# A two-layer hybrid trunk on one core: modulation sums in four partition groups, part of layer 0's modulation as steps in the prompt tile's chain, and layer 1's first three tiles in one chain

## The chip, the core and the metric

The kernel runs on one core of a Trainium2 chip. The metric is the device time of one execution in microseconds. TensorE (PE), VectorE (DVE), ScalarE (ACT), GpSimd (POOL) and SyncE (SP) each run their own instruction stream in order, and wait for each other and for DMA transfers by semaphores.

## The reference

128 prompt tokens and 512 latent tokens, 1024 wide, all float32, go through two layers. Each layer is a mixer and a mixture of experts (PEER), and each sub-layer is normed, shifted, scaled and gated by six rows of 1024 that come from a condition vector.

```
def modulation(cond, w_mod, b_mod):
    m = jax.nn.silu(cond) @ w_mod + b_mod
    return jnp.split(m[:, None, :], 6, axis=-1)
...
        sh1, sc1, g1, sh2, sc2, g2 = modulation(cond_ctx, w_mod, b_mod)
        h = modulate(xp, n1, sh1, sc1)
        if li % 2 == 0:
            out, s_f, s_b = mixer_ab(h, *mix_ab, s0, s0)
        else:
            q, k, v = attn_qkv(h, l1_w_in, l1_q_norm, l1_k_norm)
            out = context_attention(q, k, v, l1_sink) @ l1_w_out
        xp = xp + g1 * out
        xp = xp + g2 * peer(modulate(xp, n2, sh2, sc2), wq, pkeys, pu, pv)
```

The latent tokens take the same path with their own condition; in layer 1 they attend within a window of 128 to either side and to 128 cached tokens. `peer` picks 128 of 16384 experts for every token (8 heads, 16 each), takes the dot product of the token with each expert's row of `u`, and adds up the rows of `v` weighted by gate times gelu.

## The kernel before, in words

The tokens are five tiles of 128: tile 0 is the prompt, tiles 1 to 4 the latents. Two things run at once.

**The gathers.** POOL issues 1280 indirect DMAs in one fixed order, 128 "slots" for each of the ten pairs of layer and tile. One slot brings, for each of 128 tokens, one expert's `u` and `v` rows (8 KB a token) into a ring of eight places. VectorE takes the dot product (L1522), ScalarE the gelu and the gate (L1543, L1546), and VectorE (L1531) or TensorE (L1557) adds the `v` row. A ring place is free again after that.

**The stages.** A chain of stages per group of tiles computes norm, projection, mixer or attention, output, query and expert selection. The gathers of a tile can start when its selection is done. `Stage` wraps each: `rate` gives how many slots go by per unit of the stage and `lead` how many before it, and `tick` writes those slots' instructions into the engines' streams at that place. At the end of a stage all engines meet (`core.meet`). Layer 0 and the first stages of layer 1 go: prompt, first latent tile, three other latent tiles, `mod1`, then layer 1's prompt chain (`p1`), the chain of two latent tiles (`s1a`), and more.

Before the first selection there are no slots. There `Early` takes their place: 29 steps, ticked into the prompt tile's layer 0 chain by `EARLY_RATES`, norm the four latent tiles and project them (20 steps of eight matmuls, L1870), in the ring's memory, with POOL loading their weights. POOL starts the gathers after the last of them.

`modulation_stage` streams the 1024 x 6144 matrix in 12 chunks of 512 columns (2 MB each). Its matmuls have the 2 condition vectors as stationary and the chunk as moving operand. These lines of SP's stream set when a chunk is loaded; they are the same before and after:

```
            for n in range(CHUNKS + 2):
                if n >= 2:

                    sp.wait_ge(add_done, n - 1)
...
                if n < CHUNKS:
                    if n >= WSLOTS:
                        sp.wait_ge(mm_done, n - WSLOTS + 1)
                    sp.dma_start(w[:, n % WSLOTS].rearrange("p k n -> p (k n)"), wv[n]).then_inc(w_in[n % WSLOTS], 16)
```

Of the kernel before, what the change touches and what calls it, by code (L numbers as in the profile page):

```python
# [19 lines left out]
ALU = mybir.AluOpType  # L20
# [3 lines left out]
P = 128  # L24
D = 1024
# [215 lines left out]
def modulation_stage(core, layer, tag, rate=None):  # L241

    nc, a = core.nc, core.a
    CH, WSLOTS = 512, 2
    CHUNKS = MODW // CH
    with Stage(core, tag, CHUNKS, rate) as s:
        w = s.sb("w", [P, WSLOTS, DK, CH])
        cond = s.sb("cond", [P, DK, 2])
        gate = s.sb("gate", [P, DK, 2])
        act_c = s.sb("silu", [P, DK, 2])  # L250
        m = s.sb("m", [2, 2, CH])
        ps = s.ps("ps", [P, 2, CH])
# [9 lines left out]
        def _(sp):  # L262
            with nc.allow_non_contiguous_dma(reason="two vectors laid onto partitions"):
                sp.dma_start(cond[:, :, 0], a["c_ctx"].rearrange("(k p) -> p k", p=P)).then_inc(cond_in, 16)
                sp.dma_start(cond[:, :, 1], a["c"].rearrange("o (k p) -> p (o k)", p=P)).then_inc(cond_in, 16)
            wv = a[f"l{layer}_w_mod"]
            bias = a[f"l{layer}_b_mod"]
            for n in range(CHUNKS + 2):
                if n >= 2:

                    sp.wait_ge(add_done, n - 1)
                    sp.dma_start(core.env["mods"][:, layer * MODW + (n - 2) * CH:layer * MODW + (n - 1) * CH],
                                 m[:, n % 2, :]).then_inc(stored[n % 2], 16)
# [7 lines left out]
            for i in range(2):  # L281
                sp.wait_ge(stored[i], CHUNKS // 2 * 16)

        @block.scalar
        def _(act):
            act.wait_ge(cond_in, 32)
            nc.scalar.activation(gate[:], cond[:], ACT.Exp, scale=-1.0).then_inc(exp_done, 1)
            for n in range(CHUNKS):
                s.tick("scalar", act, n + 1)

        @block.vector
        def _(dve):
            order = Order(dve, dve_order)
            dve.wait_ge(exp_done, 1)
            order(nc.vector.tensor_scalar_add(gate[:], gate[:], 1.0))
            order(nc.vector.reciprocal(gate[:], gate[:]))
            nc.vector.tensor_tensor(act_c[:], cond[:], gate[:], ALU.mult).then_inc(silu_done, 1)
            for n in range(CHUNKS):
                dve.wait_ge(mm_done, n + 1)
                dve.wait_ge(b_in[n % 2], n // 2 * 16 + 16)  # L300
                nc.vector.tensor_tensor(m[:, n % 2, :], m[:, n % 2, :], ps[0:2, n % 2, :], ALU.add).then_inc(add_done, 1)  # L301
                s.tick("vector", dve, n + 1)

        @block.tensor
        def _(pe):
            pe.wait_ge(silu_done, 1)
            for n in range(CHUNKS):
# [1835 lines left out]
```

## Time and profile before

| | |
|---|---|
| three runs, median (range) | 4568.01 us (4552.75 to 4571.86) |
| the profiled execution | 4567.51 us, its span 4565.7 us |
| busy: PE, DVE, ACT, POOL | 66%, 69%, 32%, 36% |
| DMA over the span | 1570.41 MB, mean 344 GB/s |
| of it the gathers' queue | 1352.35 MB |

The span is that from the first to the last instruction. Shares of busy time are means over stages with different limits; the windows below are taken at stage boundaries.

### The profile page before, as it was taken

How to read it: one execution, taken by the hardware profiler on the slowest of the kernel's cores; microseconds unless marked ns; L12 is line 12 of the kernel's file. 1: busy time of each engine (PE TensorE's matmuls, PEld its weight loads, DVE VectorE, ACT ScalarE, POOL GpSimd, SP SyncE). 2: the span in 40 equal slices, each digit the busy share in tenths (PEclk: the TensorE clock that was granted, in tenths of full speed). 3: DMA queues.
4: the chain of work that ended last, by engine and by line, in shares of the span. 5: the costliest groups of instructions: out<-in, count | busy, mean ns of one | idle time of the engine just before them, and what ended most of it. 6: DMA issues, size and time to landing. Idle time of an engine off the chain costs nothing.

```text
span 4565.7 us, 34270 instructions
## 1 busy us (share of the span) xinstructions
PE 2993.3 (66%) x9427; PEld 1582.5 (35%) x9427; DVE 3142.8 (69%) x6200; ACT 1458.3 (32%) x4102; POOL 1632.0 (36%) x1292
## 2 busy tenths in 40 slices
PE   7668655786677765556655566575678478766665
PEld 1345334345333311234323342243335353322222
DVE  0224556995799856677777677776869678766666
ACT  0211421451223321352325323262258223332232
POOL 0000222233344435343433334333433334455453
PEclk9789777898889987778877788777887789988887
DMA  6433678788899999899988999979988899999998
GB/s 236 157 108 134 237 312 354 273 319 333 344 406 387 399 386 401 333 374 418 392 350 310 368 370 398 384 278 363 418 329 299 330 417 416 381 421 422 409 422 370
DMA packets 234038, 1570.41 MB, mean 344 GB/s; under 512 B 31717, under 2 KB 36009, under 8 KB 58889
## 3 DMA queue, kind: packets, MB, share of 16 engines
q0 software_dynamic: 185472, 1352.35, 73.6%
q1 hardware_dynamic: 48392, 216.06, 12.2%
q8 instruction: 71, 1.16, 0.1%
q14 instruction: 103, 0.84, 0.0%
HBM read 1565.07 MB, written 3.24 MB: 343 GB/s over the span
## 4 chain that ended last, share of the span: by engine, by line
DMA 37%; PE 22%; DVE 22%; issue 7%; ACT 6%; POOL 2%; DVEq 1%; PEld 1%; SPq 1%; PEldq 1%; ACTq 0%; POOLq 0%
DMA core_ring<-in_l_uv,core_experts 21%; PE sum_rows L1557 6%; DVE core_ring L1522 6%; DVE core_yv L1531 4%; DMA mod_w<-in_l_w_mod 3%; PE mod_ps L312 2%; POOL core_ring L1514 2%; ACT L1543 2%; DVEq L156 1%; PE sum_rows L1870 1%; PE p_in_ps L427 1%; PE p_query_pq L1310 1%; PE s0b_out_po L498 1%; DMA p_in_w<-in_l_w_in 1%; DMA s0a_query_w<-in_l_peer_wq 1%
## 5 line engine op out<-in xcount | busy, mean ns | idle before, releaser
L1514 POOL DMA_INDIRECT core_ring<-in_l_uv,core_experts x1280 | 1627.4, 1271 | 2510.1 <-PE sum_rows L1557 1193.0
L1522 DVE CUSTOM_DVE_ANT_0 core_ring<-core_ring,core_hc 128x1024 f32<-128x1024 f32 x1280 | 1549.0, 1222 | 598.8 <-DMA core_ring<-in_l_uv,core_experts 413.6
L1557 PE MATMUL sum_rows<-core_ring,core_diag 128*128 128x512 f32 x2772 | 1539.3, 700 | 632.3 <-ACT core_diag L1549 536.0
L1557 PEld LDWEIGHTS sum_rows<-core_ring,core_diag 128*128 128x128 f32 x2772 | 571.6, 221 | 1495.5 <-ACT core_diag L1549 860.5
L1543 ACT ACTIVATE core_wt<-core_wt 128x1 f32<-128x1 f32 x1280 | 257.5, 201 | 1888.6 <-DVE core_wt L1522 1768.4
L1531 DVE SCALAR_TENSOR_TENSOR core_yv<-core_ring,core_wt,core_yv 128x1024 f32<-128x1024 f32 x587 | 751.7, 1281 | 37.8 <-ACT core_wt L1546 36.5
L1546 ACT ACTIVATE core_wt<-core_wt,core_gates 128x1 f32<-128x1 f32 x1280 | 376.8, 294 | 64.8
L1549 ACT ACTIVATE core_diag<-core_ident,core_wt 128x128 f32<-128x128 f32 x693 | 278.2, 401 | 22.6
L312 PE MATMUL mod_ps<-mod_w,mod_silu 128*2 128x512 f32 x384 | 180.6, 630 | 67.4 <-DMA mod_w<-in_l_w_mod 67.4
L1543 ACT ACT_TABLE_LOAD x117 | 150.1, 1283 | 12.3 <-SPq L166 6.4
L1870 PE MATMUL sum_rows<-core_ring 128*128 128x416 f32 x320 | 118.4, 529 | 2.5 <-ACTq L151 1.5
L301 DVE TENSOR_TENSOR mod_m<-mod_m,mod_ps 2x512 f32<-2x512 f32 x24 | 16.2, 675 | 144.3 <-PE mod_ps L312 144.3
L312 PEld LDWEIGHTS mod_ps<-mod_w,mod_silu 128*2 128x2 f32 x384 | 32.6, 88 | 214.4 <-issue 160.6
L1522 DVE DVE_READ_ACCUMULATOR2_ANT core_wt<- 128x1 f32 x1280 | 104.0, 81 | 0.0
L1811 POOL DMA_DIRECT2D core_ring<-in_l_w_in x5 | 2.7, 538 | 274.6 <-PE sum_rows L1870 274.6
L1234 ACT ACT_TABLE_LOAD x72 | 92.4, 1283 | 16.2 <-SPq L166 10.6
L1310 PE MATMUL s0b_query_pq<-s0b_h_hT,s0b_query_w 128*128 128x384 f32 x256 | 88.0, 507 | 9.1 <-DMA s0b_query_w<-in_l_peer_wq 6.6
L1310 PE MATMUL p_query_pq<-p_h_hT,p_query_w 128*128 128x128 f32 x512 | 65.3, 290 | 29.3 <-DMA p_query_w<-in_l_peer_wq 29.3
L1870 PEld LDWEIGHTS sum_rows<-core_ring 128*128 128x128 f32 x320 | 61.6, 195 | 54.7 <-issue 54.0
L1310 PEld LDWEIGHTS p_query_pq<-p_h_hT,p_query_w 128*128 128x128 f32 x512 | 62.7, 204 | 33.9 <-DMA p_query_w<-in_l_peer_wq 33.4
L1310 PE MATMUL s1c_query_pq<-s1c_h_hT,s1c_query_w 128*128 128x256 f32 x256 | 61.3, 401 | 12.4 <-DMA s1c_query_w<-in_l_peer_wq 6.8
L1310 PEld LDWEIGHTS s0b_query_pq<-s0b_h_hT,s0b_query_w 128*128 128x128 f32 x256 | 50.5, 199 | 46.7 <-issue 8.1
(733 smaller groups left out, 3166.4 us busy)
## 6 DMA issues: line engine op xcount, KB each, us to landing
mod_w<-in_l_w_mod SPq DMA_DIRECT2D x24, 2048.0 KB, 9.3
core_ring<-in_l_uv,core_experts POOLq DMA_INDIRECT x1280
p_query_w<-in_l_peer_wq SPq DMA_DIRECT2D x32, 512.0 KB, 4.5
core_ring<-in_l_w_in POOLq DMA_DIRECT2D x5, 1664.0 KB, 7.5
p_in_w<-in_l_w_in SPq DMA_DIRECT2D x5, 1664.0 KB, 6.9
p_out_w<-in_l_w_out SPq DMA_DIRECT2D x8, 1024.0 KB, 10.3
s0a_query_w<-in_l_peer_wq SPq DMA_DIRECT2D x16, 512.0 KB, 10.3
s0b_query_w<-in_l_peer_wq SPq DMA_DIRECT2D x16, 512.0 KB, 7.9
```

Of the source, the lines that this page charges most:

```text
L156: dve.drain().then_inc(meeting, 1)
L312: mm = nc.tensor.matmul(ps[0:2, n % 2, :], act_c[:, k, :], w[:, n % WSLOTS, k, :], start=(k == 0), stop=(k == DK - 1))
L1234: nc.scalar.activation(sc[:, n % 2, 0:w], sc[:, n % 2, 0:w], ACT.Exp, bias=mx[:, n % 2:n % 2 + 1], accum_out=den[:, t % 2, head:head + 1]) ...
L1310: mm = nc.tensor.matmul(pq[:, n % 2, 0:tok], w[:, n % w_slots, k, :], hT[:, k, :], start=(k == 0), stop=(k == DK - 1))
L1514: nc.gpsimd.indirect_dma_start(self.ring[:, r, :], None, core.a[f"l{layer}_uv"], bass.IndirectOffsetOnAxis(ap=self.experts[:, t, n:n + 1], ...
L1522: nc.vector.tensor_tensor_reduce(self.ring[:, r, 0:D], self.ring[:, r, 0:D], self.hc[:], 1.0, 0.0, ALU.mult, ALU.add, self.wt[:, r:r + 1]) ...
L1531: nc.vector.scalar_tensor_tensor(self.yv[:], self.ring[:, r, D:], self.wt[:, r:r + 1], self.yv[:], ALU.mult, ALU.add).then_inc(self.used[r ...
L1543: nc.scalar.activation(self.wt[:, r:r + 1], self.wt[:, r:r + 1], ACT.Gelu_apprx_tanh).then_inc(self.gelu_done, 1)
L1546: nc.scalar.activation(self.wt[:, r:r + 1], self.wt[:, r:r + 1], ACT.Copy, scale=gate).then_inc(self.wt_done, 1)
L1549: nc.scalar.activation(self.diag[:, r, :], self.core.env["ident"][:], ACT.Copy, scale=self.wt[:, r:r + 1]).then_inc(self.diag_done, 1)
L1557: mm = nc.tensor.matmul(self.py[:, c * 512:(c + 1) * 512], self.diag[:, r, :], self.ring[:, r, D + c * 512:D + (c + 1) * 512], start=False ...
L1870: mm = nc.tensor.matmul(self.ps[:, i % 2 * 512:i % 2 * 512 + self.CH], self.hT[:, k, t * P:(t + 1) * P], w[:, k, :], start=(k == 0), stop= ...
```

## The change

Four things are changed.

The matmuls of a modulation chunk: the stationary operand is widened with zeros to 32 columns, and the eight k-blocks write into four partition groups of PSUM by k modulo 4 (`quarter_sums`). ScalarE copies the result (`part`), and one more matmul with a constant 128 x 2 matrix (`fold`) adds the groups.

`modulation_stage` for layer 0 does 4 of the 12 chunks, with four weight slots in place of two, and loads the tokens as well; `load_stage` is gone. The other 8 chunks are 11 new steps at the start of `Early` (40 steps now), with new `EARLY_RATES`; POOL loads the weights and stores the rows.

Layer 1's prompt tile and first two latent tiles go as one chain (`joined_rows`, `joint_experts`, `JOINT_RATES`): one norm, one projection, one output stage and one query stage for the group; QK and attention stay apart. Tile 2's slots of layer 0 are finished before this chain, and not in the middle of `p1`.

Stages can now hold rows of both conditions.

```diff
-def modulation_stage(core, layer, tag, rate=None):
+def modulation_stage(core, layer, tag, silu, chunks, w_slots=2, rate=None, tokens_too=False):
...
         @block.vector
...
-            for n in range(CHUNKS):
-                dve.wait_ge(mm_done, n + 1)
-                dve.wait_ge(b_in[n % 2], n // 2 * 16 + 16)
-                nc.vector.tensor_tensor(m[:, n % 2, :], m[:, n % 2, :], ps[0:2, n % 2, :], ALU.add).then_inc(add_done, 1)
-                s.tick("vector", dve, n + 1)
+            for n in range(chunks + 1):
+                if n < chunks:
+                    if rate:
+                        dve.wait_ge(mm_done, n + 1)
+                    s.tick("vector", dve, n + 1)
+                if n:
+                    i = n - 1
+                    dve.wait_ge(fold_mm, i + 1)
+                    dve.wait_ge(b_in[i % 2], i // 2 * 16 + 16)
+                    nc.vector.tensor_tensor(m[:, i % 2, :], m[:, i % 2, :], ps[0:2, i % 2, :], ALU.add).then_inc(add_done, 1)
 
         @block.tensor
         def _(pe):
-            pe.wait_ge(silu_done, 1)
-            for n in range(CHUNKS):
-                pe.wait_ge(w_in[n % WSLOTS], n // WSLOTS * 16 + 16)
+            def fold(n):
+                pe.wait_ge(part_done, n + 1)
                 if n >= 2:
                     pe.wait_ge(add_done, n - 1)
-                for k in range(DK):
-                    mm = nc.tensor.matmul(ps[0:2, n % 2, :], act_c[:, k, :], w[:, n % WSLOTS, k, :],
-                                          start=(k == 0), stop=(k == DK - 1))
-                mm.then_inc(mm_done, 1)
-                s.tick("tensor", pe, n + 1)
+                nc.tensor.matmul(ps[0:2, n % 2, :], env["fold"][:], part[:, n % 2, :], start=True, stop=True).then_inc(fold_mm, 1)
+
+            pe.wait_ge(silu_done, 1)
+            if tokens_too:
+                pe.wait_ge(fold_in, 16)
+            for n in range(chunks):
+                pe.wait_ge(w_in[n % w_slots], n // w_slots * 16 + 16)
+                if n >= 2:
+                    pe.wait_ge(part_done, n - 1)
+                quarter_sums(nc, pm[:, n % 2, :], silu, w[:, n % w_slots]).then_inc(mm_done, 1)
+                if rate:
+                    s.tick("tensor", pe, n)
+                if n:
+                    fold(n - 1)
+            s.tick("tensor", pe, chunks)
+            fold(chunks - 1)
+
+
+def quarter_sums(nc, out, silu, w):
+
+    for k in range(DK):
+        lo = 32 * (k % 4)
+        mm = nc.tensor.matmul(out[lo:lo + 32, :], silu[:, k, :], w[:, k, :], start=(k < 4), stop=(k >= 4))
+    return mm
...
     def load(self):
...
+            for n in range(chunks):
+                if n >= 2:
+                    pool.wait_ge(self.mod_mm, n - 1)
+                pool.dma_start(self.mod_w[n % 2], wv[first + n]).then_inc(self.mod_w_in[n % 2], 16)
+                if n >= 5 and n % 2:
+                    store((n - 5) // 2)
+            pool.wait_ge(self.mod_mm, chunks)
...
-EARLY_RATES = {"norm": (0.0, None, 1), "in": (1.4, None, 1), "decay": (1.0, None, 1), "gla": (0.75, None, 1), "pool": (0.0, None, 1),
-               "out": (0.0, None, 1), "query": (0.0, None, 0), "select": (0.5, None, 0)}
+EARLY_RATES = {"norm": (1.0, None, 2), "in": (1.2, None, 1), "decay": (1.0, None, 1), "gla": (1.0, None, 1), "pool": (1.0, None, 1),
+               "out": (0.5, None, 1), "query": (0.25, None, 0), "select": (0.6, None, 1)}
...
+JOINT_RATES = {"norm": (3.0, PE_4, 5), "in": (2.3, PE_0, 4), "qk": (4.0, PE_4, 5), "attend": (1.5, PE_2, 0), "out": (4.0, PE_0, 4),
+               "query": (2.2, PE_0, 2), "first select": (2.0, PE_8, 3), "select": (2.1, PE_8, 3)}
...
-            layer1_rows(core, "s1a", latents[:half], pr, LATENT_RATES)
-            qk_stage(core, "s1a_qk", latents, list(range(half)), pr, qT, kT, vc, LATENT_RATES["qk"])
-            attention_stage(core, "s1a_attend", latents, [0], pr, qT, kT, vc, env["h"], PROMPT_RATES["attend"])
-            first_experts(core, "s1a", first, 1, PROMPT_RATES)
+            joined_rows(core, "j1", prompt, p_pr, latents[:half], pr, JOINT_RATES)
+            qk_stage(core, "p1_qk", prompt, [0], p_pr, turned_queries(p_pr), p_kT, None, JOINT_RATES["qk"])
+            qk_stage(core, "s1a_qk", latents, list(range(half)), pr, qT, kT, vc, JOINT_RATES["qk"])
+            attention_stage(core, "p1_attend", prompt, [0], p_pr, turned_queries(p_pr), p_kT, None, env["h"], JOINT_RATES["attend"])
+            attention_stage(core, "s1a_attend", latents, [0], pr, qT, kT, vc, env["h"], JOINT_RATES["attend"])
+            joint_experts(core, "j1", [0, first], 1, 4, JOINT_RATES, spare)
```

TensorE's rows at the start of the program, before:

```order
L304 UNCONDITIONAL_BRANCH
L312 MATMUL mod_ps<-mod_w,mod_silu 2x512 x96
L159 UNCONDITIONAL_BRANCH x2
L388 UNCONDITIONAL_BRANCH
L395 MATMUL p_norm_ps<-core_ident,core_h 128x128 x8
```

And of the changed kernel; L350 is `quarter_sums`, L328 and L1851 are folds, `sum_rows` is the PSUM tile that the early steps use, and the silu vectors and the early chunks lie in `core_ring`:

```order
L322 UNCONDITIONAL_BRANCH
L350 MATMUL mod_pm<-mod_w,core_ring 32x512 x16
L328 MATMUL mod_ps<-mod_part,core_fold 2x512
L350 MATMUL mod_pm<-mod_w,core_ring 32x512 x8
L328 MATMUL mod_ps<-mod_part,core_fold 2x512
L350 MATMUL mod_pm<-mod_w,core_ring 32x512 x8
L328 MATMUL mod_ps<-mod_part,core_fold 2x512 x2
L159 UNCONDITIONAL_BRANCH
L1992 UNCONDITIONAL_BRANCH
L350 MATMUL sum_rows<-core_ring 32x512 x16
L414 UNCONDITIONAL_BRANCH
L421 MATMUL p_norm_ps<-core_ident,core_h 128x128 x8
```

Each fold stands behind the quarter sums of the next chunk, and the sums of two early chunks stand ahead of the norm's transposes.

VectorE's rows at the start of layer 1's modulation, before; L1522 and L1531 are a slot's dot product and row addition, L301 adds a chunk's sum to the bias:

```order
L296 RECIPROCAL mod_gate<-mod_gate 128x16
L297 TENSOR_TENSOR mod_silu<-mod_cond,mod_gate 128x16
L301 TENSOR_TENSOR mod_m<-mod_m,mod_ps 2x512
L1522 ISA core_ring,core_wt<-core_ring,core_hc 128x1024
L1522 ISA core_wt 128x1
L1531 SCALAR_TENSOR_TENSOR core_yv<-core_ring,core_wt,core_yv 128x1024
```

And of the changed kernel, from the fourth slot of this stage on; L1552, L1561 and L320 are the same three:

```order
L1552 ISA core_ring,core_wt<-core_ring,core_hc 128x1024
L1552 ISA core_wt 128x1
L1561 SCALAR_TENSOR_TENSOR core_yv<-core_ring,core_wt,core_yv 128x1024
L1552 ISA core_ring,core_wt<-core_ring,core_hc 128x1024
L1552 ISA core_wt 128x1
L1561 SCALAR_TENSOR_TENSOR core_yv<-core_ring,core_wt,core_yv 128x1024
L320 TENSOR_TENSOR mod_m<-mod_m,mod_ps 2x512
```

Before, a chunk's add came first and then the slots; now the slots of the next chunk, which wait for its matmuls, come ahead of the add.

TensorE's rows from the prompt's query to its selection in layer 0, before (L1870 is a projection step):

```order
L1310 MATMUL p_query_pq<-p_h_hT,p_query_w 128x128 x128
L159 UNCONDITIONAL_BRANCH
L1355 UNCONDITIONAL_BRANCH
L1359 MATMUL p_select_pscore<-p0q_keys,p0q_qT 128x128 x16
L1870 MATMUL sum_rows<-core_ring 128x416 x80
```

And of the changed kernel (L1971 is the projection step), from the last quarter of the query on:

```order
L1340 MATMUL p_query_pq<-p_h_hT,p_query_w 128x128 x32
L1971 MATMUL sum_rows<-core_ring 128x416 x8
L1992 UNCONDITIONAL_BRANCH x2
L1971 MATMUL sum_rows<-core_ring 128x416 x8
L1385 UNCONDITIONAL_BRANCH
L1389 MATMUL p_select_pscore<-p0q_keys,p0q_qT 128x128 x16
L1971 MATMUL sum_rows<-core_ring 128x416 x48
```

Four projections now stand within the query, one ahead of the scores and six behind them, where ten stood.

## Rows read from the trace of the kernel before

**Rows 1.** The page: the span, then groups (count | busy us, mean ns | idle).

```profile
span 4565.7 us, 34270 instructions
...
L1514 POOL DMA_INDIRECT core_ring<-in_l_uv,core_experts x1280 | 1627.4, 1271 | 2510.1 <-PE sum_rows L1557 1193.0
L1522 DVE CUSTOM_DVE_ANT_0 core_ring<-core_ring,core_hc 128x1024 f32<-128x1024 f32 x1280 | 1549.0, 1222 | 598.8 <-DMA core_ring<-in_l_uv,core_experts 413.6
...
mod_w<-in_l_w_mod SPq DMA_DIRECT2D x24, 2048.0 KB, 9.3
```

**Rows 2.** Windows of the start: length, busy us by engine, PEclk, DMA share, GB/s.

```profile
0.00:117.40 117.40, 85.59 (x192) 15.81 (x192) 8.71 (x15) 1.50 (x2) 0.20 (x4) 0.97 0.64 238
117.40:134.90 17.50, 1.97 (x8) 1.57 (x8) 4.21 (x6) 4.00 (x6) 2.84 (x5) 0.50 0.90 359
134.90:185.80 50.90, 36.34 (x114) 20.24 (x115) 12.23 (x14) 10.59 (x18) 0.00 (x0) 0.87 0.46 173
185.80:213.80 28.00, 21.91 (x64) 12.52 (x63) 2.08 (x3) 7.98 (x12) 0.00 (x0) 0.71 0.05 16
213.80:339.60 125.80, 84.61 (x371) 52.37 (x369) 35.96 (x61) 14.16 (x24) 1.06 (x2) 0.82 0.29 105
339.60:375.30 35.70, 31.66 (x256) 31.47 (x256) 0.00 (x0) 4.43 (x16) 0.00 (x0) 0.87 0.75 266
375.30:443.20 67.90, 65.56 (x208) 36.85 (x208) 44.72 (x218) 7.80 (x14) 0.53 (x1) 1.00 0.07 26
sum 443.20, PE 327.65 PEld 170.83 DVE 107.91 ACT 50.45 POOL 4.63; mean PE 46.81 PEld 24.40 DVE 15.42 ACT 7.21 POOL 0.66
```

**Rows 3.** Timeline of the start, PE and SP: start us, us, instruction, idle before.

```profile
10.32 15.95 PE L312 MATMUL mod_ps<-mod_w,mod_silu 128*2 128x512 f32 x32 [10.32 <-DMA mod_w<-in_l_w_mod]
20.45 0.35 SPq L277 DMA_DIRECT2D mod_w<-in_l_w_mod  x1
28.14 9.17 PE L312 MATMUL mod_ps<-mod_w,mod_silu 128*2 128x512 f32 x21 [1.86 <-DMA mod_w<-in_l_w_mod]
117.62 0.33 SPq L354 DMA_DIRECT2D p_norm_gain<-in_l_norm  x1
```

**Rows 4.** Timeline, PE and DVE: matmul groups, and the selection's last instruction.

```profile
375.80 3.40 PE L1359 MATMUL p_select_pscore<-p0q_keys,p0q_qT 128*128 128x128 f32 x29
379.04 56.03 PE L1870 MATMUL sum_rows<-core_ring 128*128 128x416 f32 x160
...
508.34 1.09 PE L604 MATMUL s_decay_pc<-s_mix_pr,s_decay_ku 128*64 128x128 f32 x16
...
424.64 0.29 DVE L1447 TENSOR_TENSOR core_gates<-p_select_ts,p_select_gs 128x128 f32<-128x128 f32 x1
```

**Rows 5.** Windows with L1522 alone: length, DVE busy (records), PEclk, DMA share, GB/s.

```profile
1644.50:1802.80 158.30, 40.22 (x66) 0.82 0.94 388
1802.80:2254.10 451.30, 170.40 (x280) 0.79 0.93 377
1880.70:1990.70 110.00, 41.25 (x69) 0.65 0.85 328
2254.10:2813.20 559.10, 201.83 (x333) 0.79 0.90 362
3738.40:3979.00 240.60, 111.13 (x185) 0.92 0.98 399
4068.90:4148.50 79.60, 39.46 (x65) 0.81 1.01 422
```

**Rows 6.** Timeline of layer 1's modulation, DVE, SP and PE.

```profile
1773.30 0.68 DVE L301 TENSOR_TENSOR mod_m<-mod_m,mod_ps 2x512 f32<-2x512 f32 x1 [5.44 <-PE mod_ps L312]
1773.91 1.21 DVE L1522 CUSTOM_DVE_ANT_0 core_ring<-core_ring,core_hc 128x1024 f32<-128x1024 f32 x1
...
1776.25 1.21 DVE L1522 CUSTOM_DVE_ANT_0 core_ring<-core_ring,core_hc 128x1024 f32<-128x1024 f32 x1
...
1794.71 0.68 DVE L301 TENSOR_TENSOR mod_m<-mod_m,mod_ps 2x512 f32<-2x512 f32 x1 [5.77 <-PE mod_ps L312]
...
1774.28 0.35 SPq L277 DMA_DIRECT2D mod_w<-in_l_w_mod  x1
...
1785.92 8.76 PE L312 MATMUL mod_ps<-mod_w,mod_silu 128*2 128x512 f32 x16 [5.79 <-DMA mod_w<-in_l_w_mod]
```

More of the change, by code:

```diff
@@ L337, in norm_stage @@
     x, h, ident = env["x"], env["h"], env["ident"]
-    c = cond_of(tiles)
+    conds = sorted({cond_of([t]) for t in tiles})
+    row_of = [conds.index(cond_of([t])) for t in tiles]
     NT = len(tiles)
@@ L403, in projection_stage @@
     n_chunks = n_out // chunk
+    rows = out if isinstance(out, list) else [out[:, t, :] for t in range(NT)]
     with Stage(core, tag, n_chunks * NT, rate) as s:
@@ L447, in _, with output_stage @@
                 s.tick("vector", dve, i + 1)
-def output_stage(core, tag, tiles, layer, rows, w_dram, rate=None, w_slots=4):
+def output_stage(core, tag, tiles, layer, rows, w_dram, rate=None, w_slots=4, rT=None):
     nc, env = core.nc, core.env
     x, ident = env["x"], env["ident"]
-    c = cond_of(tiles)
+    conds = sorted({cond_of([t]) for t in tiles})
     NT = len(tiles)
@@ L1629, in _ @@
             def _(sp):
+                if layer == 0 and c == 0:
+                    core.env["early"].wait_rows(sp, 3)
                 sp.dma_start(self.g2[:], broadcast_row(core.env["mods"][c, base:base + D])).then_inc(g_in, 16)
@@ L1804, in _, with store @@
             pool.wait_ge(core.meeting, met)
+            first, chunks, wv = self.MOD_FIRST, self.MOD_CHUNKS - self.MOD_FIRST, a["l0_w_mod"]
+            for i, row in enumerate(self.mod_rows):
+                pool.dma_start(row, a["l0_b_mod"][(2 + i) * D:(3 + i) * D].partition_broadcast(2)).then_inc(self.bias_in, 16)
+            def store(i):
+                pool.wait_ge(self.add_done, 2 * i + 2)
+                pool.dma_start(mods[:, (2 + i) * D:(3 + i) * D], self.mod_rows[i]).then_inc(self.stored[i], 16)
+            for n in range(chunks):
+                if n >= 2:
+                    pool.wait_ge(self.mod_mm, n - 1)
[3 more added lines that the diff above has]
+            pool.wait_ge(self.mod_mm, chunks)
             pool.dma_start(self.gain, broadcast_row(a["l0_norm1"])).then_inc(self.rows_in, 16)
@@ L1811, in _ @@
                 pool.dma_start(self.w[n % 2], a["l0_w_in"][n]).then_inc(self.w_in[n % 2], 16)
+                if n == 1:
+                    store(2)
+                    store(3)
+            for i in range(4):
+                pool.wait_ge(self.stored[i], 16)
             pool.wait_ge(self.out_done, 5 * len(self.tiles))
     def step(self, name, eng, n):
+        if n < self.MOD_STEPS:
+            self.mod_step(name, eng, n)
+            return
+        n -= self.MOD_STEPS
         nc, x, h = self.core.nc, self.core.env["x"], self.core.env["h"]
@@ L1935, in layer1_rows, with joined_rows @@
         projection_stage(core, f"{tag}_in", NT, hT, a["l1_w_in"], IN1, IN1 // 4, pr, rates["in"])
+def joined_rows(core, tag, some, some_pr, others, others_pr, rates):
+    a = core.a
+    tiles = some + others
+    NT = len(tiles)
+    with Stage(core, f"{tag}_atth") as t:
+        hT = t.sb("hT", [P, DK, NT * P])
+        norm_stage(core, f"{tag}_norm", tiles, 1, a["l1_norm1"], 0, hT, rates["norm"])
+        rows = [some_pr[:, i, :] for i in range(len(some))] + [others_pr[:, i, :] for i in range(len(others))]
+        projection_stage(core, f"{tag}_in", NT, hT, a["l1_w_in"], IN1, IN1 // 4, rows, rates["in"])
 def turned_queries(pr):
```

179 lines of the change are left out of this document (119 added, 60 removed).

## The prediction

> **What bounds the kernel now.** I read the page first. Of 4565.7 us, the 1280 gathers are the bulk: each brings 128 rows of 8 KB (1.05 MB), POOL issues it, and VectorE needs 1.22 us for its dot product [rows 1]. Near the end only gathers run: 79.6 us hold 65 dot records, two to a slot, so 32 slots, 2.49 us each, at 422 GB/s and a DMA share of 1.01 [rows 5]. From the first gather on, DMA is the bound, and every stage laid over the gathers costs its own bytes plus the time in which DMA idles. Before the first gather nothing of this runs: the windows of the start [rows 2] show 443.2 us, with a DMA share of 0.64 in the modulation and 0.05 to 0.90 after it, TensorE being the busiest engine (327.65 us). So there are three places: the start, layer 1's modulation (158.3 us, DMA share 0.94) and layer 1's two first chains (451.3 and 559.1 us, shares 0.93 and 0.90) [rows 5].
>
> **Place 1: the start.** The modulation and the load end with the next stage's first issue, at 117.6 us [rows 3]. When do they end now? The code lets SP issue chunk n only when the sum of chunk n-2 is added, and the order shows that fold n-2 now stands behind the quarter sums of chunk n-1. So after the first two chunks there is one load in flight, four slots or two. One chunk: the quarter sums are 16 matmul records. Do four column groups run side by side? No row has four of them. With 64 columns at alternating places, 16 records of 128 columns took 1.09 us, while 29 on the whole array took 3.40 us: 0.07 against 0.12 us a record [rows 4], so two groups do. I take four (3.5 us a chunk at half clock, which short bursts get in the rows with PEclk 0.50 [rows 2]; 21 records took 9.17 us at full clock, 0.437 each, so 16/4 x 0.87); one after another they cost 7.0 us [rows 3]. Chunk 0 lands at 10.3 us, chunk 1 at 2.1 MB / 422 GB/s later, 15.3. Then 3.5 for the sums, 1.7 for the fold (two records at half clock), 0.7 for the add, 0.8 to the issue: 22. A load alone takes 7.7 us (issued 20.45, used at 28.14 [rows 3]): 29.7; once more the same 14.4: 44; sums, two folds and the last add 7.6, store and meeting 2.5: 54 us. The tokens come in beneath chunk 3 and after it (2.6 MB, 6 us). That is 63 us earlier.
>
> The Trainium skill (TensorE: Matmul & The Clock Gate, Part 3, packing small matmuls) gives 2.38x for three column groups side by side, not 3x. By that a chunk's sums would be about 0.9 us longer here (an estimate from that page) and the sum some 15 us higher, with 24 chunks; no row here shows four groups.
>
> The chain of the prompt's tile then carries 11 more steps. Stage by stage against [rows 2]:
> - norm (17.5 us): TensorE's queue holds the sums of two chunks and ScalarE's holds the first part's copy ahead of the squares. Chunk 0 lands about 11 us in, 3.5 sums, 0.6 copy, 1.2 square, 1.5 root, 2.7 scaling, 2 transposes, 1 copy, then step 2 (5): 27.5. **+10**.
> - in (50.9): six quarter sums and folds (2.6 us each at full clock) stand between five projections, 5 mod chunks (10.5 MB) beside 8.5 MB of weights; the early tiles' transposes leave. **+5**.
> - decay (28.0): one projection (5.6) leaves its end, four squares enter on ScalarE, mostly beside. **-5**.
> - gla, pool, out, pnorm (125.8): 7 projections in it before, 9 now and four norms (2.5 us of VectorE each). In gla two projections remain of seven, what they free goes to the norms: +2. In pool, out and pnorm one projection in each lies at the head beneath a load, the other stands in the chain: +6, +6, +4. **+18**.
> - query (35.7, TensorE busy 31.66): four projections of 5.6 (56.03 us for ten [rows 4]). **+22**.
> - select (67.9): ten projections from 379.04 to 435.1 and one more set its end, VectorE was done at 424.9 [rows 4]. Now there are seven, one ahead of the scores (+5.6 on VectorE), so VectorE ends it. **-12**.
>
> Together +38, so gathers start 25 us earlier. Bounds: if all steps in norm, gla to pnorm and half of query's were hidden, 64; if the gla part gives no room (+10) and the sums run one after another at full clock (7.0 in place of 1.75 us for 8 chunks in the chain, of 3.5 for 4 before it: +56), a loss of 41.
>
> **Place 2: layer 1's modulation.** Here the order decides. Before, SP waited for add n-2, which needed only chunk n-2; two loads overlapped. Now VectorE waits for the sums of chunk n-1, does that chunk's 2.5 slots, and only then adds n-2, as the order below the diff shows. So load n waits for: landing of n-1, its sums 3.5, 2.5 slots of 2.34 us (dots at 1773.91 and 1776.25), so 5.9, the add and SP's issue 1.0 (1773.30 to 1774.28) [rows 6]. A load took 11.6 us here with the gathers (1774.28 to 1785.92 [rows 6]) and 7.7 alone [rows 3]. Now the slots' gathers are issued before the load and mostly done: I take 8.3. Period 18.7 us a chunk. Before, adds lie 21.4 us apart for two chunks (1773.30, 1794.71 [rows 6]), 10.7 each. Ten periods: **+80**. TensorE's saved time (7 us a chunk) buys nothing, the wait is for the load. Bounds: loads at 7.7 and sums at 1.8: +57; loads at 11.6: +113.
>
> The Trainium skill (DMA: Bandwidth & Descriptors, rules for kernel authors) says to issue a transfer early and wait for it late; this change moves the issue behind compute.
>
> **Place 3: one chain for three tiles.** Before: 451.3 + 559.1 = 1010.4 us for 306 slots (140 + 166). By rates, units and leads the joint chain takes 289: 2 (tile 2's end), norm 14, in 31, qk 13 + 21, attention 24 + 24, out 20, second norm 11, query 37, selects 45 + 47. I build it on the latent chain: 559.1; plus the prompt's qk and attention, 110.0 (34 slots); plus a second select, half of 240.6, 120.3 (46 slots); plus 43 slots more in wider stages at 2.49, 107; plus five more rows of the modulation (2.6 MB), 6; plus tile 2 finished alone before the norms, 6; less 5 for slots that fill idle DMA (share 0.90) [rows 5]: 903. Gone are 107 us, but 17 slots go to the tail, 42. **-65**. Lower bound, the matrices' bytes alone: 6.3 + 4.2 + 8.4 MB / 422 GB/s = 45, less 6: 39. Upper, no drain and 12 hidden: 78.
>
> Sum: -25 + 80 - 65 = -10, on the profiled execution's 4567.5 us (the runs' median is 4568.0): 4558 us. About 0.5% (23 us) is what a measurement of this kernel tells from none.
>
> **Rivals.**
> 1. It gains: the steps in the prompt's tile fit into idle time. For it: TensorE is idle 116 of 443 us, DMA share is 0.29 or less in half of it [rows 2]; against: query has TensorE busy 31.66 of 35.7. Then the start gives 60 in place of 25: 4523. With the matrices' chain at its upper bound 4510.
> 2. It loses: in layer 1's modulation loads keep their 11.6 us, since gathers and load share the engines as now. Place: SP's load after each add; price 10 x 3.3 = 33: 4591. From a landing time of 9.3 us on the total is above the old one; at 11.6 it is by 23. For it: both rows there; against: at the add, at most one gather of three is still under way.
> 3. The change does not do what it says: groups run one after another. That is 56 us at the start (above) and 3.5 us x 10 in layer 1: 4649. Against: two groups do run side by side [rows 4].
> 4. The load of layer 1 is not serialized (adds fall early enough): -90, so 4478. The order speaks against it.
>
> **How the numbers follow.** No change to tell 0.43 (the sum of three terms with some 12 us of doubt each); rival 1 0.28; rival 2 0.14; rival 3 0.08; rival 4 0.03; the rest 0.04. Faster by over 0.5%: 0.36 (rivals 1 and 4 and the lower edge of the forecast); within 0.42; slower 0.22. Range: from 4508, rival 1's end, to 4612, rival 2 with the start's worse half; rivals 3 and 4 are left out. The likeliest case alone: 4540 to 4580.
>
> **What would show it.** First gather issued at 418 us (before 443.2); the first stage's end at 54; matmuls of a chunk's sums starting in fours; layer 1's modulation 238 us in place of 158.3, DMA share near 0.6, one load in flight; from its end to the end of j1's last select 903 us. I am wrong if the modulation's load period stays near 11 us, or if steps make the query stage the end of more than 22 us.

## The result, and the profile after

| | before | after |
|---|---|---|
| median of four runs each, us | 4564.26 | 4598.47 |
| range, us | 4552.75 to 4571.86 | 4598.15 to 4602.54 |
| profiled execution's span, us | 4565.7 | 4597.0 |

The changed kernel takes 1.0074 of the time of the one before (95% interval 1.006 to 1.0088): it is slower by 0.74%, some 34 us. The forecast was no change, 4558 us.

The page's lines that answer to [rows 1]: the span, the gathers' issue, the dot product, and then the modulation's matmuls and its loads (the last number is the median from issue to landing).

```profile
span 4597.0 us, 33812 instructions
...
L1544 POOL DMA_INDIRECT core_ring<-in_l_uv,core_experts x1280 | 1606.0, 1255 | 2611.4 <-DVE core_yv L1561 1266.1
L1552 DVE CUSTOM_DVE_ANT_0 core_ring<-core_ring,core_hc 128x1024 f32<-128x1024 f32 x1280 | 1549.6, 1222 | 735.7 <-DMA core_ring<-in_l_uv,core_experts 409.9
...
L350 PE MATMUL mod_pm<-mod_w,mod_c_silu 128*32 128x512 f32 x192 | 41.1, 1004 | 200.7 <-DMA mod_w<-in_l_w_mod 200.7
...
mod_w<-in_l_w_mod SPq DMA_DIRECT2D x16, 2048.0 KB, 12.0
```

The gathers and dots are as they were. New is that TensorE waits 200.7 us for the loads of layer 1's modulation, where it had waited 47.6. The loads themselves are not slower than before: the 9.3 us of [rows 1] are a median over layer 0's loads too, which run without gathers. In layer 1 alone the median was 11.9 us before (its twelve loads) and is 12.0 now.

**The start.** Windows at the same stage boundaries as [rows 2]: length, busy us of PE, PEld, DVE, ACT and POOL (records), PEclk, DMA share, GB/s.

```profile
0.00:51.70 51.70, 18.16 (x72) 3.35 (x72) 3.74 (x9) 3.89 (x6) 0.91 (x6) 0.80 0.58 215
51.70:81.00 29.30, 10.98 (x58) 2.55 (x58) 4.15 (x6) 4.77 (x8) 3.82 (x8) 0.65 0.87 326
81.00:146.60 65.60, 49.11 (x174) 19.88 (x174) 5.96 (x10) 5.48 (x11) 6.70 (x13) 0.90 0.81 316
146.60:171.50 24.90, 8.63 (x33) 5.59 (x33) 3.49 (x6) 12.17 (x18) 0.00 (x0) 0.53 0.22 85
171.50:302.40 130.90, 102.70 (x434) 62.31 (x434) 45.57 (x71) 20.68 (x32) 1.09 (x2) 0.88 0.28 101
302.40:349.40 47.00, 43.45 (x260) 35.81 (x261) 0.00 (x0) 4.78 (x16) 0.53 (x1) 0.93 0.62 206
349.40:415.90 66.50, 53.63 (x206) 32.55 (x204) 44.72 (x218) 7.01 (x15) 0.01 (x1) 0.94 0.06 23
```

The first gather starts at 415.9 us where it was 443.2, a gain of 27.3.

**Layer 1.** Windows with the dot product alone (length, DVE busy and its records, PEclk, DMA share, GB/s): layer 1's modulation with tile 2's last two slots, then the joint chain to its last selection; they answer to [rows 5].

```profile
1611.10:1898.30 287.20, 42.96 (x70) 0.60 0.61 233
1898.30:2810.30 912.00, 348.95 (x575) 0.79 0.89 359
```

The modulation took 158.3 us and now, with those two slots, 287.2. Its DMA share fell from 0.94 to 0.61 and it moves 233 GB/s. The joint chain takes 912 us for 287 slots, where two chains took 1010.4 for 306.

One period of the modulation, by the timelines of TensorE, VectorE, POOL and SP (start, us, instruction, idle before it and what ended that); they answer to [rows 6]:

```profile
1687.75 3.56 PE L350 MATMUL mod_pm<-mod_w,mod_c_silu 128*32 128x512 f32 x16 [16.55 <-DMA mod_w<-in_l_w_mod]
...
1691.39 1.22 DVE L1552 CUSTOM_DVE_ANT_0 core_ring<-core_ring,core_hc 128x1024 f32<-128x1024 f32 x1 [16.01 <-PE mod_pm L350]
...
1694.09 1.68 POOL L1544 DMA_INDIRECT core_ring<-in_l_uv,core_experts  x1 [18.09 <-DVE core_yv L1561]
...
1696.44 1.68 POOL L1544 DMA_INDIRECT core_ring<-in_l_uv,core_experts  x1 [0.67 <-DVE core_yv L1561]
...
1698.42 0.67 DVE L320 TENSOR_TENSOR mod_m<-mod_m,mod_ps 2x512 f32<-2x512 f32 x1
1698.78 0.94 POOL L1544 DMA_INDIRECT core_ring<-in_l_uv,core_experts  x1 [0.67 <-DVE core_yv L1561]
...
1699.39 0.35 SPq L279 DMA_DIRECT2D mod_w<-in_l_w_mod  x1
...
1711.24 1.08 PE L350 MATMUL mod_pm<-mod_w,mod_c_silu 128*32 128x512 f32 x4 [19.08 <-DMA mod_w<-in_l_w_mod]
```

The chunk lands at 1687.75 and its sums take 3.6 us. Three slots follow on VectorE, each of which frees a place in the ring, and POOL issues a gather into it. Then come the add (1698.42) and SP's load (1699.39). The load lands at 1711.24, 11.9 us later. From landing to landing that is 23.5 us, 19.1 of them idle on TensorE. The last of the three gathers was issued 0.6 us ahead of the load, and while the load was under way the DMA engines moved two gathers' bytes beside it. Queue q0 is the gathers', q1 SP's (packets, MB, share), from 1699.4 to 1711.2 us:

```profile
q0 software_dynamic: 309, 2.14, 47.9%
q1 hardware_dynamic: 152, 2.11, 42.7%
```

The load is serialized as predicted; it is slower than predicted.

### The profile page after: what moved, and what is told of

Its sections match the earlier page's. It is cut to its first block, busy times and chain, and to the rows that moved or that the text cites. A ratio compares the mean times of both kernels' runs of the same rounds, so it can differ in the third digit from the quotient of the medians.

```text
span 4597.0 us, 33812 instructions
## 1 busy us (share of the span) xinstructions
PE 2885.1 (63%) x9215; PEld 1542.2 (34%) x9215; DVE 3144.9 (68%) x6199; ACT 1463.6 (32%) x4105; POOL 1619.0 (35%) x1308
## 4 chain that ended last, share of the span: by engine, by line
DMA 38%; DVE 23%; PE 19%; issue 7%; ACT 6%; POOL 2%; DVEq 1%; PEld 1%; SPq 1%; PEldq 1%; ACTq 0%; POOLq 0%
DMA core_ring<-in_l_uv,core_experts 23%; PE sum_rows L1587 6%; DVE core_ring L1552 6%; DVE core_yv L1561 5%; DMA mod_w<-in_l_w_mod 4%; POOL core_ring L1544 2%; ACT L1573 2%; DVEq L156 1%; PE mod_pm L350 1%; PE s0b_out_po L528 1%; DMA s0a_query_w<-in_l_peer_wq 1%; PEldq L161 1%; PE p_in_ps L454 1%; PEld p_query_pq L1340 1%; ACT L1264 1%
## 5 line engine op out<-in xcount | busy, mean ns | idle before, releaser
L1544 POOL DMA_INDIRECT core_ring<-in_l_uv,core_experts x1280 | 1606.0, 1255 | 2611.4 <-DVE core_yv L1561 1266.1
L1552 DVE CUSTOM_DVE_ANT_0 core_ring<-core_ring,core_hc 128x1024 f32<-128x1024 f32 x1280 | 1549.6, 1222 | 735.7 <-DMA core_ring<-in_l_uv,core_experts 409.9
L1561 DVE SCALAR_TENSOR_TENSOR core_yv<-core_ring,core_wt,core_yv 128x1024 f32<-128x1024 f32 x588 | 753.2, 1281 | 36.1 <-ACT core_wt L1576 35.3
L350 PE MATMUL mod_pm<-mod_w,mod_c_silu 128*32 128x512 f32 x192 | 41.1, 1004 | 200.7 <-DMA mod_w<-in_l_w_mod 200.7
L1971 PE MATMUL sum_rows<-core_ring 128*128 128x416 f32 x320 | 119.1, 530 | 5.4 <-DVEq L156 4.1
L1552 DVE DVE_READ_ACCUMULATOR2_ANT core_wt<- 128x1 f32 x1280 | 104.3, 81 | 0.0
L1264 ACT ACT_TABLE_LOAD x72 | 92.4, 1283 | 16.9 <-SPq L166 10.6
L300 ACT ACTIVATE mod_part<-mod_pm 128x512 f32<-128x512 f32 x16 | 9.6, 597 | 245.8 <-PE mod_pm L350 245.8
L1340 PE MATMUL j_query_pq<-s_att_pr,j_query_w 128*128 128x256 f32 x256 | 64.9, 416 | 31.4 <-ACT j1q_qT L1348 24.3
L350 PEld LDWEIGHTS mod_pm<-mod_w,mod_c_silu 128*32 128x32 f32 x192 | 7.0, 154 | 230.5 <-DMA mod_w<-in_l_w_mod 196.1
L1971 PEld LDWEIGHTS sum_rows<-core_ring 128*128 128x128 f32 x320 | 61.7, 196 | 56.8 <-issue 56.5
L1340 PE MATMUL s1c_query_pq<-s1c_h_hT,s1c_query_w 128*128 128x256 f32 x256 | 63.4, 410 | 14.6 <-ACT s1cq_qT L1348 8.6
L454 PE MATMUL j_in_ps<-j_in_w,j_atth_hT 128*128 128x384 f32 x192 | 65.1, 503 | 5.8 <-DMA j_in_w<-in_l_w_in 5.8
L1616 PE MATMUL sum_rows<-core_zero 128*128 128x128 f32 x160 | 34.7, 405 | 53.8 <-DVE core_x L1638 45.5
## 6 DMA issues: line engine op xcount, KB each, us to landing
core_ring<-in_l_uv,core_experts POOLq DMA_INDIRECT x1280, 12.2
```

Of the source, the lines that this page charges most:

```text
L350: mm = nc.tensor.matmul(out[lo:lo + 32, :], silu[:, k, :], w[:, k, :], start=(k < 4), stop=(k >= 4))
L454: mm = nc.tensor.matmul(ps[:, i % 4, 0:chunk], hT[:, k, t * P:(t + 1) * P], w[:, n % 2, k, :], start=(k == 0), stop=(k == DK - 1))
L1264: nc.scalar.activation(sc[:, n % 2, 0:w], sc[:, n % 2, 0:w], ACT.Exp, bias=mx[:, n % 2:n % 2 + 1], accum_out=den[:, t % 2, head:head + 1]) ...
L1340: mm = nc.tensor.matmul(pq[:, n % 2, 0:tok], w[:, n % w_slots, k, :], hT[:, k, :], start=(k == 0), stop=(k == DK - 1))
L1544: nc.gpsimd.indirect_dma_start(self.ring[:, r, :], None, core.a[f"l{layer}_uv"], bass.IndirectOffsetOnAxis(ap=self.experts[:, t, n:n + 1], ...
L1552: nc.vector.tensor_tensor_reduce(self.ring[:, r, 0:D], self.ring[:, r, 0:D], self.hc[:], 1.0, 0.0, ALU.mult, ALU.add, self.wt[:, r:r + 1]) ...
```

## The experiments

All times are medians, with the ratio to the kernel before timed on the same chip beside them. The kernel before had medians of 4557.7 to 4564.3 us there, so a difference of two medians from different comparisons is loose by up to 7 us. Stage times are those in which slots 350 to 384 go by (the expectations count from 349), the modulation of layer 1 with tile 2's last two slots (287 us in the changed kernel). A period is the mean of the ten between SP's second load of the stage and its last; in the changed kernel these are issued at 1628.6 and 1856.5 us, so it is 22.8; before the change it was 11.2. Theory A: the place of the add serializes the loads, and gathers just ahead of a load slow it. Rivals stand in each expectation.

**1. The load ahead of the store, layer 1 alone.** The diff shows the new order; the run has it for `layer == 1` only.

```diff
             for n in range(chunks + 2):
+                if n < chunks:
+                    if n >= w_slots:
+                        sp.wait_ge(mm_done, n - w_slots + 1)
+                    sp.dma_start(w[:, n % w_slots]..., wv[n]).then_inc(w_in[n % w_slots], 16)
                 if n >= 2:
                     sp.wait_ge(add_done, n - 1)
                     sp.dma_start(env["mods"][...], m[:, n % 2, :]).then_inc(stored[n % 2], 16)
```

> The changed kernel, but in layer 1's modulation SP issues the load of chunk n before it waits for the add of chunk n-2 and stores it; the load waits only for the matmuls of chunk n-2. Theory A (the loads are serialized by the place of the add, 12 us a load): two loads are in flight again, the period goes from some 22 us back to 10.7, ten periods, so slots 349 to 384 take about 175 us in place of 287, and the time is about 4490 us. Rival B (the new sums, copies, folds and the slots between them set the pace, not the loads): the stage stays above 250 us and the time above 4560.

Measured: 4505.93 us, 0.9876 (0.9833 to 0.9918). The window is

```profile
1620.90:1810.70 189.80, 43.01 (x71) 0.63 0.90 353
```

The DMA share is back at 0.90. The order of two of SP's instructions was worth some 90 us. It falls short of the 175 us: one period is 13.1 us on the mean, not 10.7. Ahead of the load of n+1 still stand the wait for the add of n-2, its store, and the bias row, which waits until the store has landed (store at 1668.11, bias row at 1676.59, load at 1676.87). Which of them costs the 2 us was not tested.

**2. The same in both stages.** The diff is the one above, for layer 0 too.

> As the run before, and the same order in layer 0's first stage, whose four chunks have four places, so all four loads are issued at once. Theory A: 8.4 MB at 422 GB/s land by 31 us, sums, fold, add, store 7 more, so the stage ends at 38 us and not at 51, and the time is 13 us below the run before, about 4477. Rival B (the chain behind it waits for something else, such as POOL's loads of the early steps): the stage ends earlier, but the first gather starts less than 5 us earlier.

Measured: 4494.39 us, 0.9865 (0.9825 to 0.9906). The first stage ended at 40 us, not at 51.7; the fourth load still stood behind the first store (SP issued it at 22.3 us). The first gather came 9.3 us earlier, so the chain behind passes it on and the rival is out. The time is 11.5 us below experiment 1's (13 expected), with intervals that overlap.

**3. Layer 1's modulation stage of before in the changed kernel.**

```diff
-            modulation_stage(core, 1, "mod1", m.sb("silu", [P, DK, 32])[:], early.MOD_CHUNKS, 2, (2.5, PE_0, 3))
+        whole_modulation_stage(core, 1, "mod1", (2.5, PE_0, 3))
```

> The changed kernel with layer 1's modulation stage as it was before the change (32 matmul records of the 2-column form, add ahead of the slots). Theory A: the stage takes 158 us again, with tile 2's last two slots 170, and the time is 4598 - 117 = 4480; within 15 us of the run with the load issued first, since TensorE's saved time buys nothing there. Rival B (part of what was lost in this stage is lost elsewhere, in the start or in the joint chain): the time stays above 4530.

Measured: 4490.16 us, 0.9843 (0.9805 to 0.9881); the stage takes 174 us. So the new form of this stage costs 108 us (4598 less 4490; 102 if each is taken against its own comparison's kernel before), and the change without it gains 1.6%. Experiment 1's time was to be within 15 us of this one and is 15.8 above.

**4. Two chains in place of the joint one.** `joined_rows` and `joint_experts` give way to the lines of before.

```diff
-            joined_rows(core, "j1", prompt, p_pr, latents[:half], pr, JOINT_RATES)
...
-            joint_experts(core, "j1", [0, first], 1, 4, JOINT_RATES, spare)
+            layer1_rows(core, "p1", prompt, pr, PROMPT_RATES)
...
+        first_experts(core, "p1", 0, 1, PROMPT_RATES)
...
+            layer1_rows(core, "s1a", latents[:half], pr, LATENT_RATES)
...
+            first_experts(core, "s1a", first, 1, PROMPT_RATES)
```

> The changed kernel with layer 1's prompt tile and first two latent tiles in two chains again, as before the change. Theory A (the joint chain gains what it saves in stages and matrices): 48 to 65 us longer, 4646 to 4663. Rival B (the gathers that it moves to the tail take up what it saves): within 15 us of the changed kernel, 4585 to 4613.

Measured: 4647.5 us, 1.0188 (1.0147 to 1.0228): the joint chain is worth 49 us (56 against each comparison's own kernel before). The modulation ends here with tile 2's last two slots still open:

```profile
1607.50:1883.30 275.80, 40.57 (x67) 0.59 0.61 233
```

**5. One partition group in place of four, layer 1.** The lines shown stand in a second function that layer 1 alone uses; the copy and the fold then read 32 rows in place of 128.

```diff
     for k in range(DK):
-        lo = 32 * (k % 4)
-        mm = nc.tensor.matmul(out[lo:lo + 32, :], silu[:, k, :], w[:, k, :], start=(k < 4), stop=(k >= 4))
+        mm = nc.tensor.matmul(out[0:32, :], silu[:, k, :], w[:, k, :], start=(k == 0), stop=(k == DK - 1))
```

> The changed kernel, but in layer 1's modulation all eight blocks of a chunk add up in the first of the four partition groups, one after another, and the fold reads that group alone. Theory A (loads are serialized, and a chunk's sums lie between two loads): the sums grow from 3.6 us to at least the 8.8 us of 16 records before the change, up to 14 at half clock, so each of ten periods grows by 5 to 10 us: slots 349 to 384 take 340 to 390 us, the time is 4650 to 4700. Rival B (sums are hidden beside slots or loads): within 15 us of the changed kernel's 4598.

Measured: 4654.68 us, 1.02 (1.0168 to 1.0233); the stage takes 350 us. TensorE's timeline has

```profile
1713.13 9.33 PE L351 MATMUL mod_pm<-mod_w,mod_c_silu 128*32 128x512 f32 x16 [16.28 <-DMA mod_w<-in_l_w_mod]
1742.11 8.50 PE L351 MATMUL mod_pm<-mod_w,mod_c_silu 128*32 128x512 f32 x16 [18.70 <-DMA mod_w<-in_l_w_mod]
```

8.5 to 9.3 us in place of 3.6, and the period grew from 22.8 to 28.4 us. The sums lie between two loads. It also shows that four groups do run side by side.

**6. No slots in layer 1's modulation.**

```diff
-            modulation_stage(core, 1, "mod1", ..., early.MOD_CHUNKS, 2, (2.5, PE_0, 3))
+            modulation_stage(core, 1, "mod1", ..., early.MOD_CHUNKS, 2)
```

> The changed kernel with no slots in layer 1's modulation; all its later slots come that much later, 29 more in the tail. Theory A (a load takes 12 us there because gathers and load share the DMA engines, and 7.7 alone): the loads take about 8 us, the period is 14 us (sums 3.6, copy and fold 1.5, add and issue 1), the stage some 170 us in place of 287; the moved slots cost 29 times 2.48 = 72, so the time is about 4555. Rival B (the load takes 12 us by itself at this place): period 18, stage 215, time about 4600 with loads of 12 us in the profile.

Measured: 4577.84 us, 1.003 (1.0014 to 1.0047). The period is 13.9 us. The DMA issues of 1650 to 1800 us have

```profile
mod_w<-in_l_w_mod SPq DMA_DIRECT2D x9, 2048.0 KB, 7.9
```

Alone, a load takes 7.9 us at this place too. What it takes beyond that, up to 12, comes with the gathers. The time is 23 us above what was expected. The expectation had missed that tile 2's slots are finished ahead of the joint chain, so that the moved slots run there and not in the tail. The window of 29 slots there is

```profile
1793.50:1875.80 82.30, 35.74 (x58) 0.83 1.01 422
```

At 82.3 us in place of the expected 72 it accounts for 10 of the 23 us. The other 13 are not explained by the place of the slots; in this execution the modulation also began 9.6 us later than in the changed kernel (first load at 1620.9 and 1611.3 us).

**7. One slot to a chunk.** The rate is 1.0 in place of 2.5.

> The changed kernel with 1 slot to a chunk in layer 1's modulation in place of 2.5, the order as it is. Theory A (the load shares the DMA engines with the gathers issued just ahead of it, byte for byte): with one gather of 1.05 MB under way the load takes 7.8 + 2.5 = 10.3 us, between the 7.8 without gathers and the 12 with two or three; the period is 3.6 + 2.3 + 2.4 + 10.3 = 18.6 us; the stage is some 45 us shorter, its 18 moved slots cost 45 in the tail, and the time stays near 4598. Rival B (any gather ahead of it costs the load its 4 us): loads of 12 us, the time near 4618.

Measured: 4595.31 us, 1.0088 (1.0054 to 1.0122); the period is 17.7 us, and the same view has

```profile
mod_w<-in_l_w_mod SPq DMA_DIRECT2D x9, 2048.0 KB, 10.4
```

So 7.9, 10.4 and 12.0 us with none, one, and two or three gathers issued ahead of the load. The first adds 2.5 us, the time in which 422 GB/s [rows 5] move its 1.05 MB. The rival's 12 us with any gather is out. By the same reckoning two gathers would make 12.9, above the 12.0 measured; what the difference comes from is not shown.

The Trainium skill (DMA: Bandwidth & Descriptors, Queues, rings and completion order) says that a DMA engine takes turns between its queues, a packet at a time. The trace of the changed kernel agrees: from 1703.0 to 1709.7 us the load and the last gather move side by side, 118 packets of the one (1.93 MB) and 111 of the other (0.90 MB).

**8. The add ahead of the slots, SP's order as changed.**

```diff
             for n in range(chunks + 1):
-                if n < chunks:
-                    if rate:
-                        dve.wait_ge(mm_done, n + 1)
-                    s.tick("vector", dve, n + 1)
                 if n:
...
                     nc.vector.tensor_tensor(m[:, i % 2, :], ...).then_inc(add_done, 1)
+                if n < chunks:
+                    if rate:
+                        dve.wait_ge(mm_done, n + 1)
+                    s.tick("vector", dve, n + 1)
```

> The changed kernel, but on VectorE the add of chunk n-1 stands ahead of the slots of chunk n, SP's order as it is. The load still waits for the sums of the chunk before, but no longer for 2.5 slots. Theory A: each period loses the 5.9 us of the slots, ten times, and a load that now starts ahead of the gathers takes 10 to 13 us: slots 349 to 384 take 220 to 240 us, time 4540 to 4555. Rival B (the slots are not in the load's path): no change, 4598. Rival C (what is saved comes back as a longer load, gathers and load then start together and land 17 us later): 270 us and more, 4580.

Measured: 4520.13 us, 0.9929 (0.99 to 0.9959); the stage takes 206 us and the period 15.0. That is better than expected, since the load itself became shorter and not longer. SP and POOL here:

```profile
1706.12 0.35 SPq L279 DMA_DIRECT2D mod_w<-in_l_w_mod  x1
...
1708.43 5.23 POOL L1544 DMA_INDIRECT core_ring<-in_l_uv,core_experts  x1 [10.17 <-DVE core_yv L1561]
```

and the DMA issues of 1650 to 1800 us:

```profile
mod_w<-in_l_w_mod SPq DMA_DIRECT2D x9, 2048.0 KB, 8.7
```

The load goes 2.3 us ahead of the first gather and takes 8.7 us (median; this one took 7.9). That gather's bytes move only behind it: from 1706.1 to 1714.0 us the gathers' queue has

```profile
q0 software_dynamic: 2, 0.01, 0.3%
```

It matters which stands first: with as many gathers behind the load as stood ahead of it before, 3.3 us are gone beside the slots' 5.9. Of these 9.2 us the period keeps 7.8: the fold, which had run beside the slots, now stands in the path. Rival C falls.

**9. The change to the start alone** (the edits of 3 and 4 together).

> The change to the start alone: layer 1's modulation and its two chains as before the change. Theory A (the parts add up): the first gather is issued at 416 us in place of 443, so the time is 27 us below the kernel before, about 4532 on its 4558. Rival B (the earlier start is given back in the following stages, as with less room for the latents' projections): less than 12 us below.

Measured: 4536.54 us, 0.9946 (0.9925 to 0.9967), 24.6 us below the kernel before (15 to 34 by the interval). The earlier start comes through almost whole.

**10. The order mended.** SP's stream and, as in 8, VectorE's; three weight places in layer 1.

```diff
+            for n in range(w_slots):
+                load(n)
+                if n < 2:
+                    bias_row(n)
...
+            for n in range(chunks):
+                if n + w_slots < chunks:
+                    load(n + w_slots)
+                sp.wait_ge(add_done, n + 1)
+                sp.dma_start(env["mods"][...], m[:, n % 2, :]).then_inc(stored[n % 2], 16)
+                if n + 2 < chunks:
+                    bias_row(n + 2)
```

> The changed kernel with the modulation's order mended: SP issues the first loads all at once and then each load as soon as the sums have left its place, ahead of the wait for the add and its store; VectorE adds chunk n-1 before the slots of chunk n; layer 1 has three weight places. Theory A: two loads in flight, so the pace of layer 1's modulation is that of the bytes (24 MB of matrix and 35 MB of gathers at 422 GB/s: 145 us, with its start and end some 165), and the first stage ends at about 38 us, first gather at 404: about 4470, 2% below the kernel before. Rival B (the sums' and folds' hand-overs bound it): 190 us as with only the load moved, 4495.

Measured: 4463.9 us, 0.979 (0.9762 to 0.9818), the best of all. The first stage ends at 37.9 us and the first gather starts at 401. The modulation of layer 1:

```profile
1596.30:1763.20 166.90, 42.87 (x70) 0.68 0.97 400
```

With a DMA share of 0.97 its bytes set its pace.

**11. The same with two places.**

> As the run before with two weight places in layer 1. Theory A: the load of n waits for the sums of n-2, which the landing of n-1 overlaps, so little is lost against three places: within 10 us of the run before. Rival B (the third place is what matters, as the load waits for the sums): 20 us or more above it.

Measured: 4479.63 us, 0.9822 (0.9791 to 0.9853); the stage takes 175 us. The third place is worth 8 us of the stage. The 16 us between the medians lie between A's 10 and B's 20; the 8 beyond the stage's are not resolved, as the two intervals overlap.

**12. The mended order with one partition group in layer 1.**

> As the run with the mended order and three places, but in layer 1 all eight blocks add up in one partition group. Theory A: the sums (8.8 us a chunk) are now shorter than the period of some 12 us and lie beside loads in flight, so the form of the sums is worth nothing here: within 8 us of the run with four groups, where with the loads serialized it was worth 56 us. Rival B (TensorE's time still counts): 20 us or more above it.

Measured: 4476.32 us, 0.9808 (0.9777 to 0.9838). The stage takes 175 us, again 8 more. Experiment 5's 56 us have become 12 (median against median), with intervals that overlap: once the loads run ahead, the form of the sums is worth little in layer 1. That TensorE's time still counts a little is not excluded, since A had said up to 8 and B 20 or more.

## Why the prediction was wrong

**The step that failed** is the load's 8.3 us in layer 1's modulation. I argued that at the add "at most one gather of three is still under way". The period of after shows two: one issued 3 us ahead of the load, one 0.6 us ahead, and 2.14 MB of gathers move while the load is under way. POOL issues a gather only when a slot's row addition has freed a place, so the gathers come as late as the slots do, and the last always stands right ahead of the add. Measured is a median of 12.0 us (mean 12.2), about what it was before the change (11.9); that was rival 2, at 14 in 100. The rest of the period was right: 10.4 us predicted, 10.6 measured (22.8 less 12.2). Ten loads 3.9 us longer are 39 of the some 44 us that the sum is off; the joint chain's shortfall is the other part. By experiments 6 to 8 the load's time follows what was issued ahead of it (shown); that the stage is in the path with all of it is shown by 1, 3 and 5.

| term | predicted | measured | from |
|---|---|---|---|
| start | -25 | -25 (first gather -27) | experiment 9, windows |
| layer 1's modulation | +80 | +108 | experiment 3 |
| joint chain | -65 | -46 to -49 | 9 against 3; 4 |
| sum | -10 | +34 | before against after |

The middle rows are differences of medians. Taken against each comparison's own kernel before, the modulation is +102 (experiment 3) or +114 (4 against 9) and the joint chain -43 (9 against 3) or -56 (4).

**The start.** The first stage ended at 51.7 us (54 said). Norm grew by 11.8 (10 said; the parts that I listed for it add up to 28.5 us and not to 27.5, so 11), decay shrank by 3.1 (5), gla to pnorm grew by 5.1 (18 said), in by 14.7 (5 said). In "in" TensorE is 12.8 us busier than in [rows 2] (49.11 against 36.34), and idle for 16.5 us where it was 14.6. I had counted on its waits to hide the quarter sums and folds; they hid nothing there. From gla to pnorm TensorE is 18.1 us busier (102.70 against 84.61) while the stages grew by 5.1: some 13 us of steps fitted into its idle time, which I had counted as chain. Query and selection together grew by 9.9 (10 said). Two errors of 10 to 13 us cancelled; the term was right partly by luck. A run whose groups add up one after another in the start was not made.

**The joint chain.** It took 912 us for 287 slots where my parts give 897 (903 less 6), and tile 2's two slots ahead of it took 11.4 us (287.2 less the 275.8 of experiment 4), not 6. The windows of the output stage and the second norm:

```profile
2322.10:2398.10 76.00, 42.86 (x176) 36.21 (x176) 57.31 (x70) 11.78 (x43) 30.33 (x21) 0.77 0.89 358
2398.10:2443.30 45.20, 14.92 (x33) 6.64 (x33) 27.79 (x37) 13.93 (x37) 11.38 (x10) 0.63 0.71 279
```

The same two stages of the latent chain before, on which I had built the sum:

```profile
2532.80:2573.10 40.30, 26.99 (x84) 19.04 (x82) 23.84 (x31) 6.70 (x24) 12.76 (x11) 0.75 0.98 386
2573.10:2602.80 29.70, 10.78 (x21) 4.96 (x22) 17.92 (x26) 9.98 (x26) 10.07 (x8) 0.67 0.80 310
```

They grew by 35.7 and 15.5 us and hold 10 and 3 slots more (20 and 11 in place of 10 and 8), which are 24.9 and 7.5 us at 2.49. So 19 us stand above the added slots, at DMA shares that fell from 0.98 and 0.80 to 0.89 and 0.71. I had charged a wider stage only its added slots, as if its own work did not grow with the tiles. That this is where the 15 us lie is read from the windows, not tested.

**The rivals.** 1: the start did not give 60 (experiment 9). 2 is what happened in layer 1. 3: four groups ran side by side, 3.6 us a chunk (3.5 said). 4: the loads were serialized. The uncertainty of some 12 us a term was too small for the load, where the far end of my own bounds (+113) was the value of a row of before. The range's lower end, 4508, is given as rival 1's, which was 4510.

The Trainium skill (DMA: Bandwidth & Descriptors, Rules for kernel authors) says to issue a transfer early and wait for it late. The prediction weighed it and priced it too low; experiment 1 measures its breach at some 90 us here.

## What to carry to other kernels

When an add or a store moves behind other work, read what else its queue holds: here SP's load stood behind a wait for a result that it did not need. Price a transfer by what is issued ahead of it at that moment, not by when that work "should" be over: a ring that refills after each use puts a gather ahead of every load that waits for the same engine. A faster form of a matmul pays only where the matmul lies between two transfers; first put the loads ahead, then see whether it is still in the path.

## What the runs showed of the hardware

- Four partition groups of 32 columns side by side: 16 matmul records of 128x512 float32 took 3.6 us where the granted clock was 0.50 and 1.92 us where it was 1.00. In one group they took 9.33 us at 0.75 and 8.50 at 0.83 (experiment 5).

```profile
1641.90:1644.00 2.10, 1.92 (x16) 0.42 (x16) 1.00 0.00 0
1666.30:1669.90 3.60, 3.59 (x16) 0.59 (x16) 0.50 0.00 0
```

The first line gives the length, PE and PEld busy and PEclk of a chunk's sums that came 1.55 us after another's, the second of sums after a long wait. At full clock that is 7.0 [rows 3] to 1.92, 3.6 times. The Trainium skill (TensorE: Matmul & The Clock Gate, Part 3) gives 2.38 times for three groups; no run here has three.

- In layer 1's modulation POOL needs 0.94 or 1.68 us to issue a gather in the changed kernel. In experiment 8 the first gather behind a load takes it 2.9 or 5.23 us, by turns. The load is not shown to be the cause: the gather that it issues at 1795.67 us takes 5.22 with no load under way. What the time goes into stays open.
